# Scan phase of a hybrid trunk: four of a tile's twelve loads change their issuing queue from SP to ACT

## The reference

```python
def step(state, inp):
    r_t, w_t, k_t, v_t, kk_t, a_t = inp
    sa = jnp.einsum("bhvk,bhk->bhv", state, -kk_t)
    state = (state * w_t[:, :, None, :] + sa[..., None] * (kk_t * a_t)[:, :, None, :]
             + v_t[..., None] * k_t[:, :, None, :])
    return state, jnp.einsum("bhvk,bhk->bhv", state, r_t)
...
_, y = lax.scan(step, state0, seq)
```

## Time and profile before

| | us |
|---|---|
| median of three runs | 3330.08 |
| lowest and highest | 3326.39, 3339.64 |
| profiled execution | 3339.32 |
| its span, first to last instruction | 3337.5 |
| PE busy | 2991.3 (90%) |
| PE weight loads busy | 2180.8 (65%) |
| DVE busy | 1453.6 (44%) |
| ACT busy | 1113.4 (33%) |
| POOL busy | 969.0 (29%) |

### The profile page before, as it was taken

One profiled execution on the slowest core, in us unless ns is written; L12 is line 12 of the kernel. 1 busy time (PEld: TensorE's weight loads), 2 busy tenths in 40 slices (PEclk: granted clock), 3 DMA queues, 4 the chain that ended last, 5 costly groups with the idle time before them and its releaser, 6 DMA issues. The chain is left out here.

```text
span 3337.5 us, 68179 instructions
## 1 busy us (share of the span) xinstructions
PE 2991.3 (90%) x26644; PEld 2180.8 (65%) x26644; DVE 1453.6 (44%) x2214; ACT 1113.4 (33%) x2268; POOL 969.0 (29%) x880
## 2 busy tenths in 40 slices
PE   6979969999999799769969799699999997998699
PEld 4767857777777544357747688577677775443577
DVE  4116733222222477377441167332222224773775
ACT  5004423333333344433250044223333333444332
POOL 4101012344444324233141000123444443232331
PEclk9999989999999779979989899899999997799799
DMA  4224533343434210176332244333344342101763
GB/s 129 68 77 136 171 111 86 99 116 112 120 109 115 78 37 7 43 224 205 110 120 68 77 150 156 111 87 102 106 116 115 112 117 79 39 7 40 223 201 114
DMA packets 421466, 358.07 MB, mean 107 GB/s; under 512 B 127656, under 2 KB 358568, under 8 KB 421160
## 3 DMA queue, kind: packets, MB, share of 16 engines
q1 hardware_dynamic: 352232, 312.93, 30.7%
q10 hardware_dynamic: 68928, 40.93, 4.5%
HBM read 222.97 MB, written 130.84 MB: 106 GB/s over the span
## 5 line engine op out<-in xcount | busy, mean ns | idle before, releaser
L130 PE MATMUL rs_acc<-h_hi,rs_w_lo 128*128 128x512 f32 x1024 | 428.2, 418 | 0.0
L128 PE MATMUL rs_acc<-h_lo,rs_w_hi 128*128 128x512 f32 x1024 | 420.0, 410 | 0.0
L124 PE MATMUL rs_acc<-h_hi,rs_w_hi 128*128 128x512 f32 x1024 | 415.6, 406 | 0.0
L124 PE MATMUL rp_acc<-h_hi,rp_w_hi 128*128 128x512 f32 x512 | 205.7, 402 | 40.7 <-PEq L121 40.7
L1802 PE MATMUL so_acc<-so_wo_hi,so_m_hi 128*128 128x512 f32 x512 | 210.3, 411 | 25.2 <-POOL so_m_lo L1724 21.3
L1516 ACT ACTIVATE fx_prob<-fx_ST 128x512 f32<-128x512 f32 (+3 forms) x320 | 155.9, 531 | 211.9 <-PE fx_ST L1378 107.0
L128 PEld LDWEIGHTS rs_acc<-h_lo,rs_w_hi 128*128 128x128 f32 x1024 | 194.2, 190 | 47.5 <-issue 6.3
L130 PEld LDWEIGHTS rs_acc<-h_hi,rs_w_lo 128*128 128x128 f32 x1024 | 194.1, 190 | 42.1
L124 PEld LDWEIGHTS rs_acc<-h_hi,rs_w_hi 128*128 128x128 f32 x1024 | 194.6, 190 | 37.8
L124 PE MATMUL pj_acc<-h_hi,pj_w_hi 128*128 128x512 f32 (+1 forms) x512 | 207.7, 406 | 5.3 <-PEq L121 5.3
L1441 DVE TENSOR_REDUCE fx_nm<-fx_SS 128x2 f32<-128x1024 f32 (+3 forms) x160 | 167.7, 1061 | 91.8 <-PE fx_SS L1353 67.2
(11 more groups left out here) (264 smaller groups left out, 6028.5 us busy)
## 6 DMA issues: line engine op xcount, KB each, us to landing
projT<-rs_stage SPq DMA_DIRECT2D x128, 256.0 KB, 2.1
pj_xb<-x SPq DMA_DIRECT2D x32, 512.0 KB, 3.5
projT<-rp_stage SPq DMA_DIRECT2D x64, 256.0 KB, 3.1
rs_raw<-w_in ACTq DMA_DIRECT2D x32, 512.0 KB
so_stage<-x SPq DMA_DIRECT2D x64, 256.0 KB, 3.0
rp_pre<-projT SPq DMA_DIRECT2D x16, 899.5 KB, 7.7
projT<-pj_stage SPq DMA_DIRECT2D x56, 256.0 KB, 2.0
rs_qx<-projT SPq DMA_DIRECT2D x112, 128.0 KB, 2.4
```

The costliest lines, as they stand in the source:

```text
L124: ins = M(acc, self.w_hi[q][:, k, 0:m], self.h_hi[:, k, cols], start=(k == 0), stop=False)
L128: M(acc, self.w_hi[q][:, k, 0:m], self.h_lo[:, k, cols], start=False, stop=False)
L130: ins = M(acc, self.w_lo[q][:, k, 0:m], self.h_hi[:, k, cols], start=False, stop=(k == KC - 1))
```

## The change

The chunk loads become a function of the issuing engine that takes two of the four buffers. SP issues those of cr only. ACT issues the four loads of bt and kt for tile t + 1 in tile t, behind the square of norm unit 1 and ahead of the evacuation of block 0, after a wait for nb_free. Those of tile 0 are issued by ACT at the head of its program, ahead of its first weight load. In the last tile nothing is loaded. The other eight loads, the semaphore and its count stay as they were.

```diff
+        def load_chunks(eng, t, e, first):
+            for n, buf in ((0, cr[e][:, :, 0, :]), (1, cr[e][:, :, 1, :]), (2, bt[:]), (3, kt[:]))[first:first + 2]:
+                for c in two:
+                    src = rw[n * GW:(n + 1) * GW, bass.ds(t * 128 + 64 * c, 64)].rearrange("(h c) t -> c h t", c=64)
+                    eng.dma_start(buf[half[c]], src).then_inc(i_in[e], 16)
...
                 if t > 0:
                     sp.wait_ge(s["nb_free"], t)
-                for n, buf in ((0, cr[e][:, :, 0, :]), (1, cr[e][:, :, 1, :]), (2, bt[:]), (3, kt[:])):
-                    for c in two:
-                        src = rw[n * GW:(n + 1) * GW, bass.ds(t * 128 + 64 * c, 64)].rearrange("(h c) t -> c h t", c=64)
-                        sp.dma_start(buf[half[c]], src).then_inc(i_in[e], 16)
+                load_chunks(sp, t, e, 0)
...
                 square(t, 1)
+                if t + 1 < NT:
+                    act.wait_ge(s["nb_free"], t + 1)
+                    load_chunks(act, t + 1, 1 - e, 2)
                 evac("s5")
...
+            load_chunks(act, 0, 0, 2)
             J.act_load(act, R_RG)
```

## The result

The changed kernel took 3358.43 us (median of 6 runs, 3353.45 to 3364.45) against 3339.26 for the kernel before beside it (3326.39 to 3341.46). The ratio on record, estimated from all these runs, is 1.0067, with a 95% interval of 1.0047 to 1.0088 (the quotient of the two medians is 1.0057). A range in brackets behind a ratio is its 95% interval, and every ratio is to the kernel before. Slower by 0.67%, where 0.63% had been forecast (3351 us against 3330.08). The kernel was timed twice more later, on other chips: 1.0034 (1.0016 to 1.0052) and 1.0024 (1.0005 to 1.0043). Weighted by their intervals the three give 1.0040, about 13 us. The first and the third interval do not overlap, so sessions differ by more than the intervals say, and 13 us is a rough figure between 8 and 22.

A forecast was written before the change was run, and what follows sets the result against it. Tensor time was taken to set the scan, with PE's repeated wait headed by ACT's evacuation. Tile terms 19.8 + 4.8 minus 4.0 at the start gave about +21 us on the median 3330.08: 3351 us, range 3331 to 3369.

The forecast's parts named there:

- the chain of waits: Scan, tiles 4 to 15: ACT's evacuation of block 0 heads SP's series, ending in PE's fourth-norm-sum wait, 38.4 us in all.
- The issues that left SP: SP's queue in the scan: four issues a tile, about 2.6 us, worth 0 in every tile but a layer's first.
- turned tiles: Scan tiles t = 4 to 15, with rotated norm units, 24 over two layers; plain ones are t = 0 to 3, eight.
- the burst did not fit: Rival, 17%: ACT's issues take 0.42 us each, the 1.8 us burst fits its 1.95 us wait; 3326 us.
- the second: Rival, 12%: ACT's burst is often slowed, mean 3.5 us, 1.6 late in turned and 1.3 in plain tiles; 3372 us.
- SP's series did not speed up: Rival, 7%, claiming the opposite: lighter SP shortens its series, PE's wait shrinks up to 0.94 us in 24 tiles; 3303 us.
- a lateness of 0.4 to 1.4 us: ACT's evacuation of block 0: range of its delay in the main forecast, 64%, giving 3336 to 3362 us.
- the evacuation at 14.4 us: Sign on ACT: first evacuation of a turned tile 14.4 us after its first transpose in place of 13.55.
- 15 to 25 us more of PE's waits: Sign on PE: waits at the fourth norm sum and for xn together larger by 15 to 25 us.
- a first transpose 2 us earlier: Sign at each scan's start: PE's first transpose comes 2 us earlier.
- The tile term: Scan tiles: late evacuation costs 0.9 us in 22 turned tiles (19.8 us) and 0.6 in 8 plain ones (4.8 us).
- The start: Start of each layer's scan: SP finishes its loads 2.6 us earlier, taken as 2.0 us gained per layer, -4.0 us.

The follow-up runs named there:

- e2: Changed kernel with the four-load burst moved behind the evacuation of block 0, ahead of the weight split; ratio 1.0176 (1.0135 to 1.0216) to the kernel before.
- e5: The changed kernel itself, run again beside a version with tile 0 loaded by SP; ratio 1.0034 (1.0016 to 1.0052) to the kernel before.
- e12: The changed kernel itself, timed a third time; ratio 1.0024 (1.0005 to 1.0043) to the kernel before.
- e9: Changed kernel with a drain on ACT between the square of unit 1 and the four loads; ratio 1.0063 (1.0038 to 1.0087) to the kernel before.
- e1: Changed kernel with ACT's four loads moved to its idle place behind the gates, before the copy of y; ratio 1.0008 (0.998 to 1.0036) to the kernel before.
- e11: Changed kernel with the burst in ACT's idle place and SP's norm-unit store and loads ahead of block 0's store; 3284.12 us, ratio 0.982 to the kernel before.

## Why the prediction was right, and where its terms were not

The direction, the place and the chain of waits held; the size of its main term did not, and the time fell close to the forecast in large part by luck. The issues that left SP lay under its wait (SP idle for 4.5 us, no gain anywhere); those that came to ACT stand ahead of the evacuation that heads the series; the burst, put at 2.8 us, measured 2.82; a loss at xn is given back at the norm sum in turned tiles and not in plain ones (e2). The rivals: the burst did not fit at 0.42 us an issue (0.637); its mean of 2.82 us is far from the 3.5 of the second; SP's series did not speed up. But the forecast was tied to a lateness of 0.4 to 1.4 us, and the lateness measured is below that. Of the signs named, the evacuation at 14.4 us, 15 to 25 us more of PE's waits and a first transpose 2 us earlier did not come (13.6, 8.4, and later).

One reading needs a correction that changes no term: the stretch called four early tiles, 519.72 to 632.88, holds three, t = 1 to 3. Two terms were mis-sized.

- *The tile term, 19.8 + 4.8 us.* The step that failed is "the issue waits for the activation's end", read from one pair of rows in the projection phase. In the scan the loads are issued while older activations still wait for the engine. The evacuation of the 22 turned tiles that load is 0.15 to 0.22 us late on average in the three traces of the changed kernel (after, e5, e12), not 0.9, and the evacuation of plain ones 0.15 to 0.36, not 0.6; PE's two kinds of stop grow by 4.6 to 8.4 us. With the drain that makes the assumption true (e9) the lateness is 1.0 and 0.8, and PE's added idle time 26.1 us against 24.6 predicted.
- *The start, -4 us.* It is +0.8. The warning stood beside the term: DMA engines 0.85 busy. The first transpose comes 11.08 us after SP's first load, against 10.66. The Trainium skill ("DMA: Bandwidth & Descriptors", section "Rules for kernel authors") says that issuing from several engines saves issue time but no bandwidth. These starts agree with it.

The pair of rows behind the first term could not carry the rule read from it. The load of 24.20 also waits for a semaphore that POOL raises when it has done w_lo, and w_lo had ended only at 23.70. And the earlier trace rows has a load issued at 469.32, just after ACT began an instruction of 1.28 us (a table load). POOL, then ACT, in the kernel before:

```profile
20.95 2.75 POOL L110 TENSOR_TENSOR pj_w_lo<-pj_raw,pj_w_hi 128x1024 fp32r<-128x1024 f32 x1 [0.27 <-POOLq L109]
...
469.21 1.28 ACT L1038 ACT_TABLE_LOAD   x1 [13.82 <-DVEq L971]
```

What the traces show, stops plus starts, is 5 to 9 us; the timings say 13 (1.0040), and the first of them 22. The rest stays open. Executions of one kernel differ by up to 40 us here, as PE's granted clock falls in different places (mean 0.924 to 0.935 over e1's executions, and the slowest had the lowest). Much of that lies where no kernel differs: the span outside tiles 0 to 15 is 2128.2 us in the trace of before and 2119.5 to 2146.9 in the five with the burst in the changed kernel's place. The narrowest of the intervals is 0.18% to either side.

## What to carry to other kernels

An engine's idle time in front of an instruction is a budget with a size. Measure the burst and where its first issue can start, against that wait, before moving work in; a place with 4.6 us idle took the same burst free (e1, e11), and the place with 2.0 us idle did not, by 5 to 10 us of PE's idle time. And when a wait is found at the end of a series, look at its head: one store and the loads behind it, ordered ahead of another store, were worth 1.5%, while moving four loads off the queue in front of it was worth nothing.

## What was not expected of the hardware

- ACT's queue issues DMAs ahead of activations that stand before them in its program: 812.37 against starts of 812.50 and 812.76. A drain stops that (817.51, behind a square that ends at 817.43). So the sentence ahead of the prediction, that nothing reorders an engine's program, holds for the order in which the queue issues; it does not say that a load waits for the computation in front of it. The Trainium skill ("Advanced Engine Details and Errata", section "Engine Queue Depths") gives ScalarE a queue of 8 instructions. The trace shows two waiting there and nothing against more.
- In e2 the plain tiles have stops of about 2.9 us, and the granted clock falls behind them. Layer 0's plain tiles t = 1 to 3 (engines' busy us, then PE's clock, DMA share, GB/s) and one of the stops:

```profile
523.57:650.63 127.06, 116.96 (x1724) 88.61 (x1723) 34.08 (x72) 35.02 (x90) 24.64 (x30) 0.96 0.29 82
...
542.34 0.71 PE L844 MATMUL rs_bk<-rs_yy,rs_xn 64*64 64x64 f32 x16 [2.96 <-PEq L652]
```

A mean of 0.96 where the earlier trace rows has 1.00: by an estimate from these two means about a twelfth of the 127.06 us ran at 1.2 instead of 2.4 GHz, and the same matmuls were busy for 4.4 us more. The price of a stop of PE was larger than its length. By single tiles, all six plain ones with t = 1 to 3 have 0.92 to 0.96 in e2, behind stops of 2.9 to 3.3 us, where the kernel before has 1.00 in all six. In the turned tiles, with stops of 2.5 to 2.9 us, the fall is not regular: 8 of the 22 up to t = 14 have 0.92 to 0.96 and the others 1.00, and in the kernel before it is 7 of 22.
